# Dealing the ranks of a mixture-of-experts gather to SBUF partitions by a count of rows per DMA engine

## What is computed

```python
logits = jnp.dot(x2, w_router).astype(jnp.float32) + b_router.astype(jnp.float32)
top_val, top_idx = lax.top_k(logits, TOP_K)            # 4 of 32
gates = jax.nn.softmax(top_val, axis=-1)
...
xb = x2[rows]                                          # rows: the tokens of one expert
gu = jnp.dot(xb, w_gu[e]) + b_gu[e]                    # 1024 x 2048 weights
gate = jnp.minimum(gate, SWIGLU_LIMIT)
up = jnp.clip(up, -SWIGLU_LIMIT, SWIGLU_LIMIT)
hmid = gate * jax.nn.sigmoid(SWIGLU_ALPHA * gate) * (up + 1.0)
return jnp.dot(hmid, w_down[e]) + b_down[e]            # 1024 x 1024 weights
...
y = jax.ops.segment_sum(y_rows * sorted_gate[:, None], sorted_tok, num_segments=N)
```

## Time and profile before

| | |
|---|---|
| median of 3 runs | 1258.81 us (1258.47 to 1260.06) |
| the profiled execution's own time | 1257.8 us |
| its span, first to last instruction | 1256.1 us |
| TensorE busy | 1187.2 us, 95% |
| VectorE, ScalarE, GpSimd busy | 84%, 75%, 12% |
| moved by DMA | 475.18 MB, mean 378 GB/s |
| mean granted TensorE clock | 0.984 |

### The profile page before, as it was taken

One profiled execution on the slowest core, in us unless ns is written; L12 is line 12 of the kernel. 1 busy time (PEld: TensorE's weight loads), 2 busy tenths in 40 slices (PEclk: granted clock), 3 DMA queues, 4 the chain that ended last, 5 costly groups with the idle time before them and its releaser, 6 DMA issues.

```text
span 1256.1 us, 35027 instructions
## 1 busy us (share of the span) xinstructions
PE 1187.2 (95%) x15369; PEld 867.3 (69%) x15369; DVE 1049.5 (84%) x1209; ACT 943.8 (75%) x1260; POOL 154.3 (12%) x141
## 2 busy tenths in 40 slices
PE   6999998899999999999999999999999999999993
PEld 3555555777777777777777777777777777777751
DVE  5564577998889889889888889988889888888868
ACT  6532313688889888888888888888888888888831
POOL 1173111110001100000000000000000111111002
PEclk9999997899999999999999999999999999999997
DMA  9852494799999999999999999999999999999983
GB/s 364 351 208 86 157 395 168 283 371 415 418 427 423 426 425 426 425 426 424 424 424 426 426 425 425 424 424 426 425 424 424 427 427 423 424 426 425 404 363 98
DMA packets 50872, 475.18 MB, mean 378 GB/s; under 512 B 8782, under 2 KB 9813, under 8 KB 24861
## 3 DMA queue, kind: packets, MB, share of 16 engines
q1 hardware_dynamic: 35432, 438.69, 83.5%
q0 software_dynamic: 8160, 18.67, 3.9%
q10 hardware_dynamic: 7124, 15.54, 3.3%
HBM read 453.17 MB, written 29.95 MB: 385 GB/s over the span
## 4 chain that ended last, share of the span: by engine, by line
PE 68%; DMA 15%; DVE 7%; ACT 4%; issue 4%; POOL 0%; SPq 0%; DVEq 0%; POOLq 0%; ACTq 0%
PE wide L1016 48%; PE pair L1016 18%; DMA ring<-in_w_gu 9%; DMA ring<-in_w_down 3%; ACT work L874 2%; DMA ring<-in_ln_b 2%; DVE work L1891 2%; PE pair L1346 2%; ACT work L904 1%; DVE ring L1993 1%; DVE ring L2018 1%; DVE ring L2016 1%; DMA ring<-in_x_t 0%; DVE ring L2005 0%; DMA work<-h_rows,work 0%
## 5 line engine op out<-in xcount | busy, mean ns | idle before, releaser
L1891 DVE SCALAR_TENSOR_TENSOR work<-ring,work 128x2048 f16<-128x2048 f32 x320 | 721.7, 2288 | 103.4 <-ACT work L874 85.5
L874 ACT ACTIVATE work<-ring 128x2048 f16<-128x2048 f32 x320 | 599.0, 1901 | 66.9 <-DMA ring<-in_w_gu 31.3
L1016 PE MATMUL wide<-work 128*128 128x96 f16 (+2 forms) x6970 | 460.3, 227 | 25.3 <-issue 14.0
L1016 PEld LDWEIGHTS wide<-work 128*128 128x128 f16 (+2 forms) x6970 | 364.2, 101 | 105.0 <-issue 35.7
L1016 PE MATMUL wide<-ring,work 128*96 128x512 f32 (+4 forms) x1024 | 333.4, 490 | 1.3 <-DMA ring<-part_rows 1.3
L1016 PEld LDWEIGHTS pair<-work 128*128 128x128 f16 (+2 forms) x6483 | 297.5, 101 | 33.5 <-issue 23.4
L1016 PE MATMUL pair<-work 128*128 128x96 f16 (+3 forms) x6483 | 304.2, 208 | 7.0 <-DVE work L1629 1.6
L1016 PEld LDWEIGHTS wide<-ring,work 128*96 128x96 f32 (+4 forms) x1024 | 131.8, 135 | 176.5 <-issue 123.3
L671 POOL DMA_INDIRECT work<-h_rows,work x32 | 52.0, 1624 | 497.5 <-PE pair L1346 257.6
L684 POOL DMA_INDIRECT part_rows<-work x30 | 35.8, 1194 | 362.6 <-ACT work L934 350.5
L934 ACT ACTIVATE work<-wide,work 96x1024 f32<-96x1024 f32 x30 | 33.2, 1107 | 57.2 <-PE wide L1016 57.2
(11 more groups left out here) (207 smaller groups left out, 577.3 us busy)
## 6 DMA issues: line engine op xcount, KB each, us to landing
ring<-in_w_gu SPq DMA_DIRECT2D x128, 2048.0 KB, 27.9
ring<-in_w_down SPq DMA_DIRECT2D x64, 2048.0 KB, 31.9
part_rows<-work ACTq DMA_DIRECT2D x1, 10240.0 KB, 36.4
ring<-part_rows SPq DMA_DIRECT2D x5, 2048.0 KB, 31.9
ring<-in_w_in SPq DMA_DIRECT2D x3, 2048.0 KB, 10.2
ring<-in_w_out SPq DMA_DIRECT2D x2, 2048.0 KB, 10.6
h_rows<-work ACTq DMA_DIRECT2D x1, 2560.0 KB, 8.7
ring<-h_rows SPq DMA_DIRECT2D x5, 512.0 KB, 24.2
```

Of the source, the lines that this page charges most:

```text
L874: act.activation(whi[buf(n, p)], packed(s, p), ACT.Copy, scale=W_UP).then_inc(hi_done, 1)
L1016: return pe.matmul(out, w, x, start=start, stop=stop, skip_group_check=True)
L1891: dve.scalar_tensor_tensor(wlo[buf(n, p)], packed(s, p), W_UP, whi[buf(n, p)], ALU.mult, ALU.subtract).then_inc(split_done, 1)
```

## The change

The table is no longer made by eight copies of a regular pattern but by an order that a greedy count makes while the kernel is built. `reader(place)` is the DMA engine to which the code counts the gather of a place, `writer(place)` the one for the scatter of the packed row that comes from it. Each of the engines in `LADEN` starts with a count of four rows, the others with none. Rank by rank, the place is taken whose two engines have the lowest sum of counts (the lowest place among equals), and both counts go up by one. The result is written on GpSimd with 96 memsets of one column each into a new tile, `dealt_rank`, right after the other constants, and VectorE copies it into `iota16` with one copy behind a wait for the new semaphore `dealt`. Nothing else differs.

```diff
+LADEN = (4, 5, 6, 7, 12, 13, 14, 15)
+HANDICAP = 4
...
+        dealt_rank = take(BLK // 2).bitcast(F16)
...
+        def deal():
+
+            load, order = [HANDICAP if q in LADEN else 0 for q in range(16)], []
+            left = [place for place in range(P) if place % 4 < 3]
+            while left:
+                best = min(left, key=lambda place: (load[reader(place)] + load[writer(place)], place))
+                left.remove(best)
+                order.append(best)
+                load[reader(best)] += 1
+                load[writer(best)] += 1
+            return order
+
+        def reader(place):
+            return 8 * (place // 64) + place // 4 % 8
+
+        def writer(place):
+            return place // 8
...
+            for i, place in enumerate(deal()):
+                at = place // 4 * 3 + place % 4
+                last = pool.memset(dealt_rank[:, at:at + 1], float(i + 1))
+            last.then_inc(dealt, 1)
...
             step(dve.memset(iota16, -1.0))
-            from_rank = iota1[:, 0:BLK].rearrange("p (d x a c e) -> p d x a c e", d=3, x=2, a=2, c=4)
-            to_place = iota16.rearrange("p (a b c e d) -> p a b c e d", a=2, b=2, c=4, e=2)
-            for b in range(2):
-                for odd in range(2):
-                    for a in range(2):
-                        step(dve.tensor_copy(to_place[:, a, b, :, odd, 0:3].rearrange("p c d -> p d c"),
-                                             from_rank[:, :, b ^ odd, a, :, odd]))
+            dve.wait_ge(dealt, 1)
+            step(dve.tensor_copy(iota16.rearrange("p (g d) -> p g d", d=4)[:, :, 0:3],
+                                 dealt_rank.rearrange("p (g d) -> p g d", d=3)))
```

More of the change, by code:

```diff
@@ L310, in build @@
         place_in = [sem(f"place_in{t}") for t in range(RUN)]
-        zeroed, tok_known = sem("zeroed"), sem("tok_known")
+        zeroed, tok_known, dealt = sem("zeroed"), sem("tok_known"), sem("dealt")
         end_tok_known, end_hot_made = sem("end_tok_known"), sem("end_hot_made")
```

## The result

The changed kernel takes 1264.22 us (median of 6 runs), the kernel before 1259.36 us beside it (6 runs): a ratio of 1.0041, 95% interval 1.0029 to 1.0053. The forecast was 1253.3 us, 5.5 us faster than before, with a range up to 1260.5 us; the kernel became 4.9 us slower and lies outside it. The profiled execution has a span of 1260.8 us for 1256.1 us.

A forecast was written before the change was run, and what follows sets the result against it. The slowest DMA engine was taken to set the end. From 1257.8 us profiled, 5.5 us (middle of 3.8 to 7.4) came off, giving 1252.3; 1.0 us for the runs' median made 1253.3 us, range 1250.0 to 1260.5 us.

The forecast's parts named there:

- What bounds the kernel: Weight streaming and the end: all 16 DMA engines full, and the slowest one sets the end of the kernel.
- The 8.45 us: At the end loads, the mean DMA engine is through 8.45 us ahead of the last: the most a deal could win.
- A surplus beside the rows, on eight engines, from the instruction fetches: On the DMA queues: 124 instruction packets at 1.13 us each, 17.5 us or 102 rows on each of eight engines.
- L: Surplus of a laden DMA engine, in rows over the run: 59 from the kernel's end, 102 from the fetches.
- If all of them fell on the eight engines of `LADEN`: Premise placing all instruction packets on the listed DMA engines; the new deal then gains 3.8 to 7.4 us.
- the surplus is not where the change thinks: Rival: the DMA surplus lies on engines outside `LADEN`, or there is none; about 5.1 us slower, 1262.9 us; chance 0.18.
- Only two engines slow (7 and 15): Rival: only these DMA engines carry the surplus; nothing won, 1257.8 us; chance 0.14, shared with any case of nothing won.
- Compute as the bound: Rival: TensorE's waits behind 920 us have causes other than DMA; half the gain, 2.7 us, 1255.1 us; chance 0.08.
- A nearly perfect deal: Rival: the DMA engines end almost together; 8.45 us gained, 1249.4 us; chance 0.07.
- The rest of the edit hidden: GpSimd's 96 memsets, 3 to 10 us, fit in a 36.27 us wait; VectorE's single copy wins nothing.
- What would show it: Signs in the later profile: weight landing time 900 to 1100 us about 33 us if right, above 40 if surplus elsewhere.
- VectorE's wait for `in_ln_b`: Sign at the kernel's end: this wait was to shrink from 7.40 us to 2 to 5 us.

The follow-up runs named there:

- e1: The changed kernel with a handicap of 0 instead of 4 for the engines in `LADEN`: 1258.85 us, ratio 0.9995 to the kernel before.
- e2: The changed kernel with `LADEN` = (5, 6, 9, 10, 11, 12, 13, 14), same handicap of 4: 1252.81 us, ratio 0.9955 to the kernel before.
- e11: The kernel before with one of three products of the gate and up matmuls left out, all data moving as before: 1253.15 us, ratio 0.9947.
- e12: The kernel of e2 with one of three products of the gate and up matmuls left out: 1253.26 us, ratio 0.9951 to the kernel before.
- e7: The changed kernel with `LADEN` = (5, 6, 9, 11, 12, 13, 14, 15), so 15 in place of 10 in e2's list: 1264.59 us, ratio 1.0036 to the kernel before.
- e3: The changed kernel with the old order of places, still written by 96 memsets, semaphore and copy: 1259.67 us, ratio 1.0004 to the kernel before.

## Why the prediction was wrong

*What bounds the kernel* was right: the slowest DMA engine. Where the work as a whole stays the same, a lead or lag at the landings came out in the time nearly one for one (the table: 5.1 us further behind the mean made 4.9 us; 4.9 us nearer made 5.9 us). The 8.45 us by which the mean engine was through earlier than the last is 9.8 us in the landings.

*A surplus beside the rows, on eight engines, from the instruction fetches*: right. e1 and e2 show the surplus, e11 and e12 that it is the fetches. Its size, taken between L = 59 and L = 102 rows, is 90 to 105. The row was priced at 0.172 us and is 0.16 us; the fetch at 1.13 us and costs 1.55 us where the packet beside it is slowed, four times of five.

*The step that failed* is the sum's "If all of them fell on the eight engines of `LADEN`": the last engine was then engine 4 with 299 + L before, and 256 + L against 336 after. Engine 4 is not laden. Of the eight in `LADEN`, five are (5, 6, 12, 13, 14); 9, 10 and 11 are laden and weren't in it. By the rows the last engine before was then engine 5 with 295 + L, and after it is engine 11 with 331 + L, 36 rows more: 5.8 us, where 4.9 us were measured. The mean engine didn't change.

*The rival "the surplus is not where the change thinks"* gave the sign and the size, 5.1 us later, for 4.9 us measured. Its example of 0 to 3 and 8 to 11 was not the set, so that 5.1 us came so near is partly luck. Its mechanism asks only for one laden engine among those that receive rows; e7 shows that one is enough. In that light its chance of 0.18 was too low. Eight engines of sixteen had to be right at once, and no row named even one of them. The sixteen landings of the kernel before could have shown that the last engine is 9.8 us behind; which engines are laden took kernels with other tables.

*Only two engines slow (7 and 15)*: falls. By the fit neither is laden, and in e7, where 15 gets few rows, it can only be the one that is 9.9 us ahead. This case doesn't bear out the rule of the Trainium skill ("DMA: Bandwidth & Descriptors", "Latency and other measured facts") that these two are usually the slow ones: in the numbering of `reader` the slow ones were 5, 6 and 9 to 14. *Compute as the bound* falls with e2 and e12. *A nearly perfect deal* was not reached, but e2 wins 5.9 of its 8.45 us. *The rest of the edit hidden* was right: e3.

*What would show it*: the text had named "above 40 us" to landing and a falling share at the end as the sign of a surplus elsewhere. They came as 40.1 us and 0.75. Of the two only the share is a good sign: e7, as slow as the change, has 0.70 but only 36.0 us to landing in that stretch, and e1, no slower than before, has 39.3 us. VectorE's wait for `in_ln_b` did not tell the cases apart: 6.15 us after, 5.96 us in e2, 7.40 us before.

What stays open: that each of 5, 6, 9, 11, 12, 13 and 14 is laden rests on the fit and on the tight landings of e2; only 10 and 15 were swapped by themselves. That the fetches run on these engines is concluded from the landings, as no record of a packet names its engine. Why the fetches go to these eight isn't known, nor whether they would in another program.

## What to carry to other kernels

When all DMA engines are full and one load spreads over all of them, the time is that of the last engine. Here levelling paid only with every engine of the list right, and one wrong engine cost as much as three. So measure the load of each engine first, from the spread of one load's landings in kernels with different deals, then deal. The instruction stream is part of that load: in this kernel, where weights stream at full rate, leaving matmuls out relieved the DMA engines that fetch their instructions, though TensorE itself wasn't the bound.

## What the runs showed of the hardware

- The packets of the instruction queue `q8` follow TensorE's instructions: 124 packets for 30,738 matmuls and weight loads, and 92 when 8,192 of these are gone, 256 to a packet of 16 KB. By the landings of eight kernels they fall on eight of sixteen DMA engines, here 5, 6 and 9 to 14.
- A fetch costs its engine up to 1.55 us beside streaming weights, 1.07 us of its own and, four times of five, 0.5 us in a neighbouring packet: 32 of these packets fewer, of 50,872 in all, moved the end by 6.2 us.
- A load's landings can lie 27 us apart while the mean share of the DMA engines reads 1.00 and the rate 420 GB/s: the averages say nothing of imbalance until the queues run dry.
